# SSD scan on one core: the C-B product goes through ScalarE and GpSimd instead of VectorE

## The reference

```python
def ssd_mixer(z, xbc, dt, conv_w, conv_b, dt_bias, a_log, d_skip, norm_w):   # 8 heads, 2 groups, chunks of 64
    ...
    lmat = lower_exp_diff(a_cs)                        # exp(a_cs[i] - a_cs[j]) for j <= i, else 0
    scores = jnp.einsum('bclhn,bcshn->bhcls', cc, bc) * lmat
    y_diag = jnp.einsum('bhcls,bcshp->bclhp', scores, xc)
    ...                                                # chunk_states, scan over the chunks, y_off
    y = (y_diag + y_off).reshape(bsz, t, SSD_HEADS, SSD_HEAD_DIM) + xs * d_skip[:, None]
    g = y.reshape(bsz, t, SSD_DIM) * jax.nn.silu(z)    # then a group norm

def first_block(x, ...):
    ...
    att = swa_sink_alibi(a_q, a_k, a_v, attn_sinks[l])
    ssd = ssd_mixer(s_z, s_xbc, s_dt, ...)
    gdn = gdn_mixer(g_qkv, g_z, g_b, g_a, ...)
    mix = jnp.concatenate([att, ssd, gdn], axis=-1) @ w_out[l]
    x = x + rmsnorm(mix, post_mix_norm[l])
    ...                                                # gated feed-forward, then a second layer
```

## Time and profile before

| quantity | value |
|---|---|
| time, median of three runs | 2302.89 us |
| span of the profiled execution, first to last instruction | 2301.8 us |
| TensorE busy | 2126.3 us (92%) |
| VectorE busy | 1236.5 us (54%) |
| ScalarE busy | 864.8 us (38%) |
| GpSimd busy | 890.8 us (39%) |
| mean granted TensorE clock | 0.973 |
| the stretch with SSD scan and windowed attention | about 386 to 513 us |

### The profile page before, as it was taken

One profiled execution on the slowest core, in us unless ns is written; L12 is line 12 of the kernel. 1 busy time (PEld: TensorE's weight loads), 2 busy tenths in 40 slices (PEclk: granted clock), 3 DMA queues, 4 the chain that ended last, 5 costly groups with the idle time before them and its releaser, 6 DMA issues. The chain is left out here.

```text
span 2301.8 us, 29448 instructions
## 1 busy us (share of the span) xinstructions
PE 2126.3 (92%) x10799; PEld 1783.6 (77%) x10799; DVE 1236.5 (54%) x1827; ACT 864.8 (38%) x1562; POOL 890.8 (39%) x612
## 2 busy tenths in 40 slices
PE   6999998868998999999999968889999999999997
PEld 6788877758886788888877757768888888888886
DVE  4443503866537843444489897679995245110232
ACT  4332216456324434343444544238774122000112
POOL 1232331331345688888832643220000333333334
PEclk9999998889999999999999988999999999999999
DMA  4111310011132122222274534200001111111131
GB/s 147 46 46 46 83 55 19 19 46 38 43 104 85 35 55 65 74 64 74 82 248 142 188 100 147 93 28 1 1 1 33 46 46 37 55 46 47 55 119 73
DMA packets 181824, 157.43 MB, mean 68 GB/s; under 512 B 27589, under 2 KB 147121, under 8 KB 181553
## 3 DMA queue, kind: packets, MB, share of 16 engines
q1 hardware_dynamic: 163904, 119.05, 17.4%
q10 hardware_dynamic: 17776, 36.51, 4.3%
HBM read 134.03 MB, written 21.50 MB: 68 GB/s over the span
## 5 line engine op out<-in xcount | busy, mean ns | idle before, releaser
L1118 POOL TENSOR_SCALAR w_hi<-w_raw 128x1024 fp32r<-128x1024 f32 x91 | 106.0, 1165 | 942.3 <-issue 893.6
L1230 PE MATMUL gemm<-h_hi,w_hi 128*128 128x512 f32 x1072 | 422.4, 394 | 5.6 <-POOL h_lo L1147 5.6
L1232 PE MATMUL gemm<-h_hi,w_lo 128*128 128x512 f32 x1072 | 418.2, 390 | 0.0
L1231 PE MATMUL gemm<-h_lo,w_hi 128*128 128x512 f32 x1072 | 418.0, 390 | 0.0
L1230 PEld LDWEIGHTS gemm<-h_hi,w_hi 128*128 128x128 f32 x1072 | 202.0, 188 | 49.6 <-issue 9.1
L1232 PEld LDWEIGHTS gemm<-h_hi,w_lo 128*128 128x128 f32 x1072 | 201.6, 188 | 42.5
L1231 PEld LDWEIGHTS gemm<-h_lo,w_hi 128*128 128x128 f32 x1072 | 202.1, 189 | 40.4
L1121 POOL TENSOR_TENSOR w_lo<-w_raw,w_hi 128x1024 fp32r<-128x1024 f32 x91 | 230.0, 2527 | 7.6
L870 POOL TENSOR_TENSOR w_lo<-wsum,w_hi 128x512 fp32r<-128x512 f32 x122 | 165.6, 1358 | 83.1 <-ACT w_hi L1682 77.8
L1682 ACT ACTIVATE w_hi<-wsum 128x512 fp32r<-128x512 f32 x155 | 98.1, 633 | 142.0 <-PE gemm L1310 60.8
L1308 PE MATMUL gemm<-h_hi,w_hi 128*128 128x512 f32 x320 | 124.5, 389 | 0.0
(11 more groups left out here) (435 smaller groups left out, 4662.9 us busy)
## 6 DMA issues: line engine op xcount, KB each, us to landing
w_raw<-in_ffn_w_down SPq DMA_DIRECT2D x132, 256.0 KB, 3.1
w_raw<-in_w_in SPq DMA_DIRECT2D x60, 512.0 KB, 3.8
w_raw<-in_ffn_w_gate SPq DMA_DIRECT2D x22, 512.0 KB, 4.0
w_raw<-in_ffn_w_up SPq DMA_DIRECT2D x22, 512.0 KB, 4.1
w_raw<-in_w_out SPq DMA_DIRECT2D x16, 512.0 KB, 3.8
xin<-in_x SPq DMA_DIRECT2D x8, 512.0 KB, 6.9
x<-in_x ACTq DMA_DIRECT2D x1, 4096.0 KB, 15.7
x_spill<-x ACTq DMA_DIRECT2D x2, 2048.0 KB, 6.6
```

What stands on the lines that cost most here:

```text
L1118: gp.tensor_scalar(hi[:], raw[key % 4][:], 1.0, 0.0, ALU.mult, ALU.add).then_inc(pool_hi, 1)
L1230: mm(o, hi[:, k, m], act[0][:, k, t], start=k == 0, stop=False)
L1231: mm(o, hi[:, k, m], act[1][:, k, t], start=False, stop=False)
L1232: last = mm(o, lo[:, k, m], act[0][:, k, t], start=False, stop=k == kt - 1)
```

## The change

The two VectorE multiplications of `sg` are removed. ScalarE copies the two products of a chunk from PSUM into a new SBUF tile `cbs` (two buffers), one instruction of 128x256, and that copy frees the bank. GpSimd then multiplies `cbs` into E in SBUF, two instructions of 128x512, and raises a new semaphore, `e_ready`. TensorE waits for `e_ready` before `yd`, and ScalarE waits for it before it writes the same `cbs` buffer again. Each engine does its part at the place of `sg` in the common list.

```diff
--- before.py
+++ after.py
@@ -506,6 +506,7 @@
         upper = con[:, C_UP:C_UP + P]
         blk = con[:, C_BLK:C_BLK + P]
         identb = sbuf("identb", [P], 105.5, BF16)
+        cbs = [sbuf(f"cbs{i}", [2, P], 103.5 + i) for i in range(2)]
         negb = sbuf("negb", [P], 105.75, BF16)
         cols = sbuf("cols", [112], 106)
         bias16 = sbuf("bias16", [16], 106.5)
@@ -680,7 +681,7 @@
             "rec_vn", "rec_S", "mix_ssd", "mix_gdn", "gated", "sq_gdn", "kbv_ready", "resid_done", "d_hi", "d_low", "d_sum", "d_used", "d_copied", "w_sum_v", "rope_done", "gb_used",
             "mean_done", "ln_done", "a2_max", "split_hi", "split_lo", "y_done", "yT_hi", "yT_lo", "final_done",
             "ga_gated", "pt_used", "fold_ready", "tok_sq", "kx_ready", "ed_ready", "o_summed", "sq_ssd",
-            "ssd_rs", "gdn_rs", "pool_step", "sq_part", "rs_ready",
+            "ssd_rs", "gdn_rs", "e_ready", "pool_step", "sq_part", "rs_ready",
             "low_ready", "acc_gained", "comb_sum", "comb_add", "comb_hi", "comb_lo", "w_sum", "w_quarter_hi", "t_copied", "sg_ready", "f_made", "tok_used", "ob_sq", "ob_gained")}
         z_out = [sem(f"z_out{i}") for i in range(2)]
         z_in = [sem(f"z_in{i}") for i in range(2)]
@@ -1184,6 +1185,13 @@
                     step(gp.tensor_tensor(h64(kbv[z][:, 0, :]), v_, widen(beta[:, c, :], 64), ALU.mult))
                     step(gp.tensor_tensor(h64(kbv[z][:, 1, :]), k_, widen(bge[:, c, :], 64), ALU.mult))
                     step(gp.tensor_tensor(h64(kbv[z][:, 2, :]), k_, widen(ed[:, c, 8:12], 64), ALU.mult), "kbv_ready")
+                elif kind == "sg":
+                    c, z = j, j % 2
+                    pool.wait_ge(N["ed_ready"], NT + c + 1)
+                    side_consumed(pool, (it, 0))
+                    for g in range(2):
+                        e = E[z][:, 4 * g:4 * g + 4, :]
+                        step(gp.tensor_tensor(e, e, over(cbs[z][:, g, :], 4), ALU.mult), "e_ready" if g else None)
                 elif kind == "gn":
                     pool.wait_ge(N["gdn_rs"], j + 1)
                     pool.wait_ge(zg_in, 16)
@@ -1488,7 +1496,7 @@
                             last = mm(b[:, g * 256:g * 256 + 256], BC[:, 2 + g, hslice(c)], Sst[:, g * 256:g * 256 + 256],
                                       start=True, stop=True)
                     elif kind == "yd":
-                        side_consumed(pe, (("sg", c), 0))
+                        pe.wait_ge(N["e_ready"], c + 1)
                         pe.wait_ge(N["kx_ready"], c + 1)
                         for h in range(8):
                             last = mm(b[:, h * 64:h * 64 + 64], E[z][:, h, :], xc[z][:, 0, h * 64:h * 64 + 64], start=True, stop=True)
@@ -1908,6 +1916,13 @@
                             n = slice(32 * b, 32 * b + 32)
                             m = con[:, C_B32 + 32 * b:C_B32 + 32 * b + 1]
                             step(af(d[z][:, :, n], x, ACT.Identity, scale=m), "x_exp" if i and b == 3 else None)
+                elif kind == "sg":
+                    c, z = j, j % 2
+                    if c >= 2:
+                        act.wait_ge(N["e_ready"], c - 1)
+                    b = side_product(act, (it, 0))
+                    ins = af(cbs[z][:], b[:, 0:2 * P].rearrange("p (g n) -> p g n", g=2), ACT.Copy)
+                    step.frees(ins, (it, 0))
                 elif kind == "rk":
                     z = j % 2
                     b = side_product(act, (it, "kT"))
@@ -2463,11 +2478,7 @@
                         e = Eg[z][:, 2 * p:2 * p + 2, :].unsqueeze(2).to_broadcast([P, 2, 2, P])
                         step.frees(v.tensor_tensor(SQ[c][:, 2 * p:2 * p + 2], b[:].rearrange("p (h a n) -> p h a n", h=2, a=2), e, ALU.mult), (it, f"kq{p}"))
                 elif kind == "sg":
-                    z = j % 2
-                    dve.wait_ge(N["ed_ready"], NT + j + 1)
-                    b = side_product(dve, (it, 0))
-                    step(v.tensor_tensor(E[z][:, 0:4, :], E[z][:, 0:4, :], over(b[:, 0:P], 4), ALU.mult))
-                    step.frees(v.tensor_tensor(E[z][:, 4:8, :], E[z][:, 4:8, :], over(b[:, P:2 * P], 4), ALU.mult), (it, 0))
+                    continue
                 elif kind == "inv":
                     if j == 0:
                         dve.wait_ge(w_split, job_of[rec_weight - 3] + 1)
```

## The result

The changed kernel takes 2309.57 us, the median of 6 runs (2307.71 to 2312.85, and one of 2317.87), against 2302.29 us before. The medians lie 7.3 us apart. The ratio of all runs is 1.004 with a 95% interval of 1.003 to 1.005, which is 9.2 us; it is not the ratio of the medians. The forecast was 2308.0, slower, range 2302.8 to 2311.5.

A forecast was written before the change was run, and what follows sets the result against it. No engine was taken as always last; VectorE was busy 13.8 of 16 us in passes with inverse steps. Terms 1.4 + 1.1 + 1.0 + 0.6 + 0 + 1.0 = 5.1 us on 2302.9 gave 2308.0, range 2302.8 to 2311.5.

The forecast's parts named there:

- The freed VectorE time: VectorE at `sg`: the 1.4 us removed per pass are mostly time in which it would idle, waiting for attention scores.
- The prices: New instructions: 1.28 us for each GpSimd multiplication of 128x512, 0.386 us for ScalarE's copy.
- Start-up and pass 1: First chunk: `yd(0)` starts some 4.5 us later; 3.1 fall into idle time, 1.4 us go through to the next pass.
- The stops: VectorE instructions with all operands in SBUF stand still until a GpSimd instruction is over, costing 0 to 1.1 us a wait.
- Pass 4: Two tiny VectorE instructions before attention output are held, by the second multiplication and by xc: +1.0 us.
- Pass 7: GpSimd's multiplications of E hold one or more of the three tiny VectorE instructions, 0.3 to 1.7: +1.0 us.
- passes 2, 3 and 6: Pass 2: later yo and L2531 held by the burst, +1.1 us; pass 3: 0.3 us; pass 6: 0.
- pass 5: Same pieces as pass 4 at other distances, a loss between 0 and 1.1 us, taken as 0.3 us.
- all operands in SBUF: VectorE instructions of this kind wait out a GpSimd instruction, those with a PSUM operand do not; without this 1.9 us, not 5.1.
- A: Rival: the lock hardly meets anything, leaving start-up 1.4 and pass 2 0.5, so 1.9 us: 2304.8; chance 0.25.
- B: Rival: freed VectorE time counts in passes full of VectorE work, 4.2 us faster net: 2298.7; chance 0.07.
- C: Rival: GpSimd's instruction takes 1.475, the burst reaches every tiny instruction, start-up at half clock: 10.4 us, 2313; chance 0.13.

The follow-up runs named there:

- E1: The kernel before with VectorE's multiplications of E left out, a one-column copy freeing the bank: ratio 0.9998 to before.
- E10: The changed kernel with attention's row maximum in an unused PSUM bank: 2304.93 us, ratio 1.0011 to the kernel before.
- E3: The changed kernel with GpSimd's two multiplications replaced by eight write-only memsets of 128x256: ratio 1.0015 to the kernel before.
- E5: The changed kernel with chunk 0 multiplied by VectorE from PSUM as before: ratio 1.0036 to the kernel before.
- E11: The kernel before with attention's row maximum in an unused PSUM bank, as a control: 2303.53 us, ratio 1.0002 to before.
- E9: The changed kernel itself measured again: 2310.65 us, ratio 1.0037 to the kernel before.
- E4: The changed kernel with E multiplied in four GpSimd instructions of 128x256 instead of two of 128x512: ratio 1.0031 to the kernel before.

## Why the forecast was right, and where its sum was too small

**The freed VectorE time.** Forecast: worth nothing, since VectorE waits for scores there. Shown by E1 (0.9998). The 11.4 us turned mostly into waiting: VectorE's wait for the scores was 6.7 us before and 17.1 after.

```profile
DVE asb L2424 <- PE side L1394: 6.7, 6, 3.7
```

```profile
DVE asb L2439 <- PE side L1402: 17.1, 11, 5.4
```

**The prices.** 1.28 forecast and 1.268 measured for a multiplication, 0.386 and 0.384 for the copy.

**Start-up and pass 1, +1.4.** Measured from the first xc in both kernels, `yd(0)` came 8.2 us later before and 11.9 after, 3.7 us in place of the 4.5 forecast. The difference is the stop of the earlier trace rows: before, it held the exponentials that the copy stands behind by 0.85 us, and in this execution it is not there. The masks of pass 1 ended at 19.8 and 21.2 us, 1.4 later, as forecast. The rows that answer to the earlier trace rows:

```profile
394.39 2.61 POOL L1194 TENSOR_TENSOR E<-E,cbs 128x512 f32<-128x512 f32 x2 [3.91 <-ACT cbs L1924]
...
397.10 3.65 PE L1502 MATMUL side<-xc,E 128*128 128x64 f32 x16 [4.75 <-issue]
...
400.54 1.91 PE L1410 MATMUL side<-con,asb 128*128 128x128 f32 x8
...
402.25 1.16 PE L1505 MATMUL side<-xc,Bt 128*128 128x256 f32 x4
```

After 4.75 us without work TensorE ran `yd(0)` in 3.65 us and the transposes in 1.91, nearly twice the 1.90 and 1.05 of the forecast; the granted clock was 0.50 from 397.0 to 402.2 us, the level of 1.2 GHz. Before, that level fell on st(0) (1.91 us), and here st(0) took 1.16. That the sum came out at 1.4 is therefore partly luck: its parts are others than the forecast's.

**The stops.** Pass 4 went as forecast: one tiny instruction held to the end of the second multiplication, the next through, the third held by xc, 1.1 us of standing still for a forecast delay of 1.0. Pass 7 did too, 1.1 us in one stop. The term that was mis-sized is the number of stops in the other passes. For passes 2, 3 and 6 the prediction has one late L2531, 0.3 and nothing; the profile has two stops of tiny instructions in each, 0.8 us or so apiece. In pass 1 it has none and the profile two, 1.6 us together. In pass 5 it has 0.3 and the profile nothing. For pass 2 the forecast lets the exponentials start when they did before, which puts the tiny instructions ahead of the burst. But they came later. The rows of pass 2:

```profile
416.30 2.08 PE L1505 MATMUL side<-xc,Bt 128*128 128x256 f32 x4 [1.15 <-ACT cd L1888]
...
422.67 0.39 ACT L1924 ACTIVATE cbs<-side 128x256 f32<-128x256 f32 x1
...
423.23 2.61 POOL L1194 TENSOR_TENSOR E<-E,cbs 128x512 f32<-128x512 f32 x2 [1.73 <-ACT cbs L1924]
423.27 1.24 DVE L2442 TENSOR_TENSOR amx<-amx,sinkb 128x4 f32<-128x4 f32 x1
...
424.75 1.11 DVE L2444 TENSOR_TENSOR ads<-sinkb,amx 128x4 f32<-128x4 f32 x1
```

L2442 missed GpSimd's start by 0.04 us and lost 1.1. Counted from the first xc, st(1) began 3.0 us later than before, which is the 1.4 of the start-up and the 1.6 of the stops in pass 1. It then ran at a granted clock of 0.50 (2.08 us; 1.13 in the earlier trace rows), and the masks ended 3.8 us later than before. So the stops of one pass moved the tiny instructions of the next. Taken at the two profiles, standing still in the tiny instructions and the decay was 5.0 and 8.8 us, of which 0.9 was there before, where the sum had some 3.7 (all terms but the start-up). That fits a loss of 7.3 and 8.4 us between the medians in place of 5.1.

**Which instructions are held.** The prediction says "all operands in SBUF", from one row. That is too wide. The row maximum has its operands in SBUF and took its plain 1.22 us beside the multiplications of pass 4, and a reciprocal of 128x4 at 456.57 its plain 0.18 beside a GpSimd instruction that had begun at 456.48. Held were the `tensor_tensor` instructions with two inputs in SBUF and the `tensor_scalar` with one.

**Rivals.** A (the lock hardly meets anything) fell: taking the tiny instructions out of reach gave back 5.7 us (E10). B (VectorE's time is worth something) fell with E1 for this change as made. C named the right effect, a burst that reaches the tiny instructions in nearly all passes (six of seven), by a wrong price for GpSimd.

**Left open.** The late E by itself: E3 gives 3.4 us by the ratio and E10 leaves 2.7 between the medians, with stops and waits for yo's bank in it, and E5 did not show the share of the start-up. How much of the loss and of the spread comes by way of the granted clock was not separated. The stretch in E11's profile took 130.1 us, 3.4 more than in that of before, at a ratio of 1.0002 and with none of the three tiny instructions stopped; TensorE was busy for 100.1 us in it, at 0.83, for 96.3 at 0.85 before. So a difference of some 3 us between the stretches of two profiles says little.

## What to carry to other kernels

Before giving an engine's work to another, leave it out altogether and time that: here it was worth nothing, so the freed time alone had nothing to win. When elementwise work goes from VectorE to GpSimd, look at what VectorE runs beside it: `tensor_tensor` instructions with both inputs in SBUF, and here a `tensor_scalar` too, stood still until GpSimd's was over, and a 0.16 us instruction on a critical chain pays the same price as a long one. If such work has to be on GpSimd, put one operand of the small VectorE instructions next to it into PSUM: that gave back 5.7 of 8.4 us here.

## What the runs showed of the hardware beyond that

- Between two GpSimd instructions 0.08 us apart the waiting VectorE instruction ends (463.46 in pass 4), and the next one, begun in the gap (463.50), runs its plain 0.17 us though GpSimd's begins at 463.52. The third is held again. So three tiny ones in a row cost up to two GpSimd instructions (1.24 and 1.11 us in pass 2).
- GpSimd is held as well: in E9 its xc began at 423.30 while a stopped decay was still running (to 423.77), and took 1.37 us in place of 1.04.
- A `tensor_scalar` of 4 elements per row is stopped as well (1.02 us in the earlier trace rows, 1.25 in pass 7, up to 0.40 beside memsets of 0.311 in E3); with its input in PSUM it wasn't (0.16 beside a multiplication in E10).
- GpSimd's multiplication of 128x256 took 0.746 us against 1.268 for 128x512: halving an instruction there added 0.11 us to each half, in E4.
